# Differential attention in a decoder trunk: the fourth group's values are projected beside its own heads, score halves alternate, sums of squares go inside output units

## The chip, the cores and the metric

The kernel runs on one core of one Trainium2 chip. The metric is the device time of one execution in microseconds (us), lower is better. The engines are named as in the profile: PE (TensorE matmul), PEld (TensorE weight load), DVE (VectorE), ACT (ScalarE), POOL (GpSimd), SP (SyncE, which here issues all the weight DMAs).

## The reference

A trunk of two layers on 256 tokens of width 2048, everything in float32. Layer 0 mixes with sliding-window attention, layer 1 with differential attention; each is followed by cross-attention into 256 memory tokens and a gated MLP with a width-3 convolution. The change lies in the differential attention of layer 1:

```python
def diff_attention(h, w_qkv, w_o, lq1, lk1, lq2, lk2, subln_g, lambda_init):
    qkv = h @ w_qkv                       # 16 heads, two query/key halves of 64 each, values of 128
    q, k, v = jnp.split(qkv, 3, axis=-1)
    ...
        s = jnp.einsum('bqhmd,bshmd->bhmqs', qblk, k) * scale
        s = s - slopes[None, :, None, None, None] * dist
        s = jnp.where(dist >= 0, s, NEG_INF)
        p = jax.nn.softmax(s, axis=-1)
        a = p[:, :, 0] - lam * p[:, :, 1]
        return jnp.einsum('bhqs,bshe->bqhe', a, v)
    ...
    o = rmsnorm(o, subln_g) * (1.0 - lambda_init)   # over the 128 values of a head
    return o.reshape(B, S, DIFF_HEADS * DIFF_V_DIM) @ w_o
```

## The kernel before

Weights stream in **units** of 1 MB (128 partitions x 4 x 512 float32). SP loads unit after unit into four raw slots, ACT copies a unit to its rounded high part (`hi_unit`, L226), DVE subtracts to get the low part (`lo_unit`, L234), and PE multiplies high by high, high by low and low by high (`triple`, L317 to L319). The high and low parts also have four slots: the high part of a unit may be made once the unit four places earlier has been used by PE (`units_used`), and both are made three units ahead of PE (`AHEAD = 3`). A unit is either projected with the weights stationary and 256 tokens streaming (`proj_unit`: queries, keys, output) or with the tokens stationary and 512 weight columns streaming (`token_unit`: values).

The order of the work is written out by hand for each engine, and semaphores tie the engines together. There is no scheduler. Each engine runs its own list strictly from top to bottom, so whatever stands behind an instruction that waits, waits too.

The 16 heads of the differential attention come in four groups of four. After group g's heads follows its **key-value block**: the keys of group g+1 (four units, into the PSUM pair PB), then the values of group g+1 (four units, into PD). Between and beside them:

- *Scores of a head* (`diff_scores`, L941 and L942): for each of the two halves m, on partitions 0 to 63 or 64 to 127, a matmul of 128 columns and one of 256 columns, into PC. Written in the order half 0 (128, 256), half 1 (128, 256).
- DVE adds the distance bias (L1877), takes maxima (L1883, L1884) and negates them (L1888): `diff_bias_max`. ACT takes four exponentials (L1327): `diff_exp`. DVE combines the two softmaxes (L1896 to L1908): `diff_combine`. PE transposes the probabilities (L629): `diff_turn`. ACT moves them to SBUF (L1102): `evac_probs`. PE multiplies by the values (L951 to L953): `diff_pv`. ACT moves the result (L1335): `diff_o_evac`.
- When a group's four heads are done, ACT squares the outputs (L1341), PE sums over partitions with a matrix of ones (L960, `head_norm_sums`), DVE scales the sums (L1916, `diff_norm_first`), ACT takes the root (L1345), DVE takes the reciprocal over 128x1024 (L1920) and multiplies (L1923): `diff_norm_last`. These are placed beside the next keys' units.
- The output projection of group g-1 runs in four output units beside the heads of group g (`o_unit`); DVE adds each to the residual h (L381, `add_block`).
- DVE moves the keys out of PSUM with a scale (L375, `evac_k`) and the values (L1851, L1852, `evac_v`).

Groups 1 and 2 are one hardware loop over g (`Fori(1, 3)`, L999, L1373, L1949). In it `diff_pv(g, 3)` stands right behind `diff_pv(g, 2)`, ahead of the key-value block.

The fourth group (g = 3) is written out. Its heads run beside the output units of group 2, one unit per head. Its own outputs are normalised in two halves of two heads (`half_squares` L1390, `half_norm_sums` L1018, `half_norm_first` L1964, `half_root` L1397, `half_norm_last` L1970 and L1973), split into high and low (`o_hi_half` L1132, `o_lo_half` L1566), and projected by the last four output units, of which `last_part` does a quarter at a time. `last_blocks` then needs the second half.

Of the kernel before, what the change touches and what calls it, by code (L numbers as in the profile page):

```python
# [27 lines left out]
ALU = mybir.AluOpType  # L28
# [3 lines left out]
P = 128  # L32
# [22 lines left out]
AHEAD = 3  # L55
# [6 lines left out]
B_DIFF = B_FF[0] + 3 * FF_STEPS  # L62
# [12 lines left out]
def trunk(nc, x, mem, norm_mix, norm_cross, norm_mem, norm_ffn, norm_final,  # L75
# [4 lines left out]
    with ExitStack() as ctx:  # L80
# [66 lines left out]
        PA, PB, PC, PD = pair  # L147
# [383 lines left out]
        def _(pe):  # L531
# [432 lines left out]
            def diff_turn(g, j):  # L964
                if j == 0:
                    pe.wait_ge(dif["v_evac"], g + 1)
                turn_probs(dif, g, 4, j, pbuf[:, j % 2], THREE)

            def key_value_blocks(g, b4, j0, behind):

                for kq in range(KQ):
                    proj_unit(pe, b4, j0 + kq, PB, xhi, xlo, kq, kq == 0, kq == 3)\
                        .then_inc(units_used, 1)
                    if kq == 0 and behind:
                        diff_turn(g, 3)
                        diff_pv(g, 2)
# [22 lines left out]
            with pe.Fori(1, 3) as g:  # L999
# [10 lines left out]
                diff_pv(g, 3)  # L1010
# [9 lines left out]

            b4 = B_DIFF + 14
            for j in range(3):
                diff_scores(3, j)
                o_unit(dif, 3, b4, j, j, False)
                if j >= 1:
                    diff_turn(3, j - 1)
                if j >= 2:
                    diff_pv(3, j - 2)
            diff_scores(3, 3)
            diff_turn(3, 2)  # L1030
            diff_pv(3, 1)
            diff_pv(3, 2)
            pe.wait_ge(dif["biased"], 16)
            half_norm_sums(0)
            o_unit(dif, 3, b4, 3, 3, False)
            diff_turn(3, 3)
            diff_pv(3, 3)
            half_norm_sums(1)
            last_part(dif, B_DIFF + 15, 0, 0)
            last_part(dif, B_DIFF + 15, 1, 0)  # L1040
            last_part(dif, B_DIFF + 15, 0, 1)
# [7 lines left out]
        def _(act):  # L1049
# [297 lines left out]
            def beside_key_value_blocks(g, b4, j0, behind):  # L1347
                for t in range(8):
                    hi_unit(act, b4, j0 + t + AHEAD)
                    if behind and t == 0:  # L1350
                        evac_probs(dif, g, 4, 3, 3 * P)
                        diff_o_evac(g, 2)
# [20 lines left out]
            with act.Fori(1, 3) as g:  # L1373
# [8 lines left out]
                diff_o_evac(g, 3)  # L1382
                diff_norm(g)
# [16 lines left out]
            heads_with_one_unit(3, b4, 3)  # L1400
# [3 lines left out]
            diff_exp(3, 3)  # L1404
            diff_o_evac(3, 2)
            half_root(0)
            evac_probs(dif, 3, 4, 3, 3 * P)
            diff_o_evac(3, 3)
            o_hi_half(dif, 0)
            half_squares(1)  # L1410
            half_root(1)
            o_hi_half(dif, 1)
            hi_unit(act, b4, 3 + AHEAD)
# [6 lines left out]
        def _(dve):  # L1420
# [428 lines left out]
            def evac_v(g, done):  # L1849
                dve.wait_ge(units_used, done)  # L1850
                dve.tensor_scalar(diff_v[:, 0], PD[:, 0:512], rcol[:, 1, 0:1], None, ALU.mult)  # L1851
                dve.tensor_scalar(diff_v[:, 1], PD[:, 512:1024], rcol[:, 1, 1:2], None, ALU.mult)\  # L1852
                   .then_inc(dif["v_evac"], 1)
# [12 lines left out]
            evac_v(0, 4 * B_DIFF + 12)  # L1866
# [59 lines left out]
            def beside_key_value_blocks(g, b4, j0, q_done, behind):  # L1926
# [5 lines left out]
                for t in range(8):  # L1932
# [8 lines left out]
                evac_v(g + 1, b4 * 4 + j0 + 8)  # L1941
# [7 lines left out]
            with dve.Fori(1, 3) as g:  # L1949
                b4 = g * 4 + (B_DIFF + 2)  # L1950
                for j in range(4):
# [4 lines left out]
                    diff_combine(g, j)  # L1956
                    lo_unit(dve, b4, 2 * j + 1 + AHEAD)
                add_block(dif, b4, 7, PB[:], 3)
# [8 lines left out]
            def half_norm_last(i):  # L1967
                part = q_flat[:, 512 * i:512 * i + 512]
                dve.wait_ge(dif["o_root"], GROUPS + i)
                dve.reciprocal(part, part).then_inc(dif["o_rstd"], 1)  # L1970
                dve.wait_ge(dif["o_rstd"], GROUPS + i)
# [5 lines left out]
            for j in range(4):  # L1977
                diff_bias_max(3, j)
                if j >= 1:
                    add_block(dif, b4, j - 1, pair[(j - 1) % 2][:], j - 1)  # L1980
                if j < 3:
                    lo_unit(dve, b4, j + AHEAD)
                    diff_combine(3, j)
            half_norm_first(0)
            diff_combine(3, 3)
            half_norm_last(0)
            o_lo_half(dif, 0)
            half_norm_first(1)
            add_block(dif, b4, 3, PB[:], 3)
# [49 lines left out]
```

## Time and profile before

Three runs: median 2413.57 us, lowest 2412.19, highest 2415.09.

| | us |
|---|---|
| time of the profiled execution | 2412.89 |
| its span in the profile | 2411.1 |
| PE busy | 2366.2 (98% of the span) |
| DVE busy | 1752.5 (73%) |
| ACT busy | 1183.5 (49%) |
| group 1, first score matmul to group 2's | 101.93 |
| group 2, first score matmul to group 3's | 101.92 |
| group 3, first score matmul to the first output quarter that needs its second half | 44.74 |

In these last three stretches PE is busy for 101.08, 101.07 and 41.12 us, DVE for 72.14, 70.67 and 39.39 us, and the mean granted clock of PE is 1.00, 1.00 and 0.96 of full speed. A timeline row gives start, duration, engine, line, operation, written and read tiles, shape, how many records were merged, and in brackets the idle time of the engine before it with what ended it. The time between the starts of two rows of PE, and not the sum of durations, is what a piece of work costs there, since matmuls overlap in the pipeline.

### The profile page before, as it was taken

To read this page: it belongs to the slowest core of one execution; us is meant where nothing else is said; L and a number is where in the kernel's file an instruction comes from. 1 tells how busy PE (TensorE), PEld (TensorE's weight loads), DVE (VectorE), ACT (ScalarE), POOL (GpSimd) and SP (SyncE) were. 2 spreads that over 40 slices of the span, in tenths; PEclk is the share of its full clock that TensorE was granted. 3 is DMA by queue.
4 is the path that set the end of the run, shared out by engine and by line. 5 is a ranking of instruction groups with operands and counts; after the bars stand their busy time and mean duration, and the time that the engine had idled before them with its cause. 6 is when DMAs were issued, how large, how long until landed. Compare 5 with 4: busy or idle time off the path is not lost.

```text
span 2411.1 us, 36280 instructions
## 1 busy us (share of the span) xinstructions
PE 2366.2 (98%) x14781; PEld 2104.2 (87%) x14781; DVE 1752.5 (73%) x2043; ACT 1183.5 (49%) x1363; POOL 8.6 (0%) x19
## 2 busy tenths in 40 slices
PE   6999999999999999999999999999999999999998
PEld 6898889988888888888899999889888888888887
DVE  5766667777777777777966867787766766676667
ACT  5544446554444444444545444456544444444444
POOL 1000000000000000000000000000000000000000
PEclk9999999999999999999999999999999999999999
DMA  7653433465555555555464544535555555555552
GB/s 260 210 177 106 137 110 120 160 208 192 192 184 194 187 186 189 191 191 192 157 210 158 169 160 160 174 112 180 191 198 187 182 194 188 190 187 196 189 186 96
DMA packets 211928, 424.90 MB, mean 176 GB/s; under 512 B 6896, under 2 KB 7168, under 8 KB 211200
## 3 DMA queue, kind: packets, MB, share of 16 engines
q1 hardware_dynamic: 211152, 421.69, 51.7%
q0 software_dynamic: 688, 1.96, 0.3%
q8 instruction: 66, 1.08, 0.2%
q14 instruction: 22, 0.18, 0.0%
HBM read 421.52 MB, written 2.10 MB: 176 GB/s over the span
## 4 chain that ended last, share of the span: by engine, by line
PE 95%; DVE 3%; ACT 1%; DMA 1%; issue 0%; SPq 0%; ACTq 0%; DVEq 0%
PE pair L343 33%; PE pair L345 17%; PE pair L317 14%; PE pair L319 13%; PE pair L318 13%; DVE wlo L234 1%; PE pair L629 1%; PE pair L620 0%; PE pair L640 0%; PE pair L619 0%; DMA raw<-in_x_w_kv 0%; ACT whi L226 0%; DMA raw<-in_mem 0%; PE pair L641 0%; PE pair L642 0%
## 5 line engine op out<-in xcount | busy, mean ns | idle before, releaser
L234 DVE TENSOR_TENSOR wlo<-raw,whi 128x2048 fp32r<-128x2048 f32 x396 | 905.1, 2288 | 330.1 <-ACT whi L226 329.8
L226 ACT ACTIVATE whi<-raw 128x2048 fp32r<-128x2048 f32 x396 | 756.8, 1914 | 693.5 <-PE pair L345 403.7
L343 PE MATMUL pair<-xx,whi 128*128 128x512 f32 x2880 | 1002.0, 394 | 1.2
L345 PE MATMUL pair<-xx,wlo 128*128 128x256 f32 x2880 | 798.4, 277 | 0.0
L343 PEld LDWEIGHTS pair<-xx,whi 128*128 128x128 f32 x2880 | 540.0, 188 | 130.3 <-issue 5.2
L345 PEld LDWEIGHTS pair<-xx,wlo 128*128 128x128 f32 x2880 | 540.9, 188 | 0.1
L317 PE MATMUL pair<-xx,whi 128*128 128x256 f32 x1184 | 343.2, 290 | 9.9 <-DVE wlo L234 9.1
L318 PE MATMUL pair<-xx,whi 128*128 128x256 f32 x1184 | 336.5, 284 | 0.0
L319 PE MATMUL pair<-xx,wlo 128*128 128x256 f32 x1184 | 336.4, 284 | 0.0
L317 PEld LDWEIGHTS pair<-xx,whi 128*128 128x128 f32 x1184 | 228.6, 193 | 20.3 <-issue 18.7
L318 PEld LDWEIGHTS pair<-xx,whi 128*128 128x128 f32 x1184 | 228.7, 193 | 1.5 <-issue 1.2
L319 PEld LDWEIGHTS pair<-xx,wlo 128*128 128x128 f32 x1184 | 228.6, 193 | 0.0
L343 PE MATMUL pair<-oo,whi 128*128 128x512 f32 x640 | 222.6, 394 | 1.2 <-DVE h L1630 1.2
L345 PE MATMUL pair<-oo,wlo 128*128 128x256 f32 x640 | 177.3, 277 | 0.0
L317 PE MATMUL pair<-oo,whi 128*128 128x256 f32 x512 | 147.7, 289 | 1.0 <-DVE oo L1560 1.0
L343 PEld LDWEIGHTS pair<-oo,whi 128*128 128x128 f32 x640 | 120.0, 188 | 29.4 <-DVE h L1630 1.5
L319 PE MATMUL pair<-oo,wlo 128*128 128x256 f32 x512 | 144.9, 283 | 0.0
L318 PE MATMUL pair<-oo,whi 128*128 128x256 f32 x512 | 144.8, 283 | 0.0
L381 DVE TENSOR_TENSOR h<-h,pair 128x1024 f32<-128x1024 f32 x80 | 97.4, 1217 | 53.0 <-PE pair L319 52.9
L1756 DVE TENSOR_TENSOR work<-pair,work 128x512 f32<-128x512 f32 x88 | 56.7, 686 | 101.5 <-ACT work L1237 101.5
L317 PE MATMUL pair<-whi,oo 128*128 128x512 f32 x320 | 124.6, 390 | 0.0
L319 PE MATMUL pair<-whi,oo 128*128 128x512 f32 x320 | 124.6, 389 | 0.0
(204 smaller groups left out, 2684.2 us busy)
## 6 DMA issues: line engine op xcount, KB each, us to landing
raw<-in_ffn_w_up SPq DMA_DIRECT2D x176, 1024.0 KB, 5.0
raw<-in_ffn_w_down SPq DMA_DIRECT2D x88, 1024.0 KB, 5.0
raw<-in_diff_w_qkv SPq DMA_DIRECT2D x48, 1024.0 KB, 5.1
raw<-in_swa_w_qkv SPq DMA_DIRECT2D x20, 1024.0 KB, 5.1
raw<-in_x_w_kv SPq DMA_DIRECT2D x16, 1024.0 KB, 6.2
raw<-in_swa_w_o SPq DMA_DIRECT2D x16, 1024.0 KB, 5.0
raw<-in_diff_w_o SPq DMA_DIRECT2D x16, 1024.0 KB, 5.0
raw<-in_x_w_q SPq DMA_DIRECT2D x8, 1024.0 KB, 5.5
```

The source lines that it names most:

```text
L226: act.activation(whi[:, s], raw[:, s], ACT.Copy).then_inc(hi_ready, 1)
L234: dve.tensor_tensor(wlo[:, s], raw[:, s], whi[:, s].bitcast(F32), ALU.subtract)\
L317: pe.matmul(dst, ahi, bhi, start=start, stop=False, skip_group_check=True)
L318: pe.matmul(dst, ahi, blo, start=False, stop=False, skip_group_check=True)
L319: return pe.matmul(dst, alo, bhi, start=False, stop=stop, skip_group_check=True)
L343: pe.matmul(banks[m], whi[:, s, k, w], act2[:, c].rearrange("p a t -> p (a t)"), start=c == 0, stop=False, skip_group_check=True)
L345: ins = pe.matmul(banks[m][:, 0:SEQ], wlo[:, s, k, w], act2[:, c, 0], start=False, stop=last and k == 3, skip_group_check=True)
L381: return dve.tensor_tensor(part, part, src, ALU.add)
L629: ins = pe.transpose(pt_ps[:, dst_cols], src[:, src_cols], ident[:])
L1756: ins = dve.tensor_tensor(part, high, part, ALU.add)
```

## The change

1. **Score halves alternate.** The four matmuls of a head's scores are written 128 (half 0), 128 (half 1), 256 (half 0), 256 (half 1).
2. **`diff_pv(g, 3)` moves** from ahead of the key-value block to behind its first key unit for g = 1 and 2; ACT's evacuation and squares move with it. DVE's fourth `add_block` moves one `lo_unit` earlier.
3. **The value units of group 3 leave the key-value block of group 2** and stand beside group 3's first heads: two behind the scores of head 0, two behind the scores of head 1. They go into PB, where the keys of group 3 have been. The key-value block of g = 2 is left with its four key units; its `evac_k` on DVE comes at the end of that shortened block, and the high and low parts of group 2's output (`o_hi_all`, `o_lo_all`) come after it. The wait for the values moves from `diff_turn` to `diff_pv`.
4. **Group 3 is written anew** on PE, ACT and DVE. The two sums of squares stand inside output units 2 and 3, behind the first quarter of each (`o_unit_around_sums`). On ACT, `evac_probs` of head 3 stands behind `o_hi_half(0)`. On DVE, `half_norm_recip` is a function of its own. The last output unit's quarters go 0,0 0,1 1,0 1,1.
5. The loop over g = 1, 2 becomes two written-out copies on the three engines. SP's list is as before.

```diff
@@ pe: diff_scores, diff_pv, diff_turn @@
-                for m in range(2):
-                    half = slice(64 * m, 64 * m + 64)
-                    dst = PC[:, 512 * m:512 * m + 384]
-                    pe.matmul(dst[:, 0:P], q_sb[half, j, Q0], k_sb[half, j, 0:P], start=True, stop=True)
-                    ins = pe.matmul(dst[:, P:3 * P], q_sb[half, j, Q1], k_sb[half, j, :], start=True, stop=True)
+                halves = [slice(64 * m, 64 * m + 64) for m in range(2)]
+                for m, half in enumerate(halves):
+                    pe.matmul(PC[:, 512 * m:512 * m + P], q_sb[half, j, Q0], k_sb[half, j, 0:P], ...
+                for m, half in enumerate(halves):
+                    ins = pe.matmul(PC[:, 512 * m + P:512 * m + 3 * P], q_sb[half, j, Q1], k_sb[half, j, :], ...
...
+                if j == 0:
+                    pe.wait_ge(dif["v_evac"], g + 1)      # in diff_pv
...
-                if j == 0:
+                if j == 0 and g < 3:                      # in diff_turn
                     pe.wait_ge(dif["v_evac"], g + 1)
@@ pe: key_value_blocks and groups 1, 2 @@
+                        else:
+                            diff_pv(g, 3)                 # behind key unit 0
...
+                if g == 2:
+                    return
                 pe.wait_ge(dif["o_evac"], g * 4 + 4)
...
-            with pe.Fori(1, 3) as g:
+            for g in (1, 2):
...
-                diff_pv(g, 3)
                 pe.wait_ge(dif["h_added"], g * 4)
                 key_value_blocks(g, b4, 8, False)
@@ pe: group 3 @@
+            def o_unit_around_sums(nb, i):
+                pe.wait_ge(dif["h_added"], 7 + nb)
+                for k in range(4):
+                    ins = proj_part(pe, b4, nb, pair[nb % 2], ohi, olo, k)
+                    if k == 0:
+                        half_norm_sums(i)
+                ins.then_inc(units_used, 1)
+            diff_scores(3, 0); value_unit(0); value_unit(1); diff_turn(3, 0)
+            diff_scores(3, 1); value_unit(2); value_unit(3)
+            diff_scores(3, 2); diff_turn(3, 1); diff_pv(3, 0); o_unit(dif, 3, b4, 0, 0, False)
+            diff_scores(3, 3); pe.wait_ge(dif["v_evac"], 4); o_unit(dif, 3, b4, 1, 1, False)
+            diff_turn(3, 2); diff_pv(3, 1)
+            pe.wait_ge(dif["biased"], 16)
+            o_unit_around_sums(2, 0)
+            diff_turn(3, 3); diff_pv(3, 2); diff_pv(3, 3)
+            o_unit_around_sums(3, 1)
@@ act: group 3 @@
+            o_hi_all(dif, 2, "o_normed"); hi_unit(act, B_DIFF + 13, 0 + AHEAD); diff_exp(3, 0)
...
+            diff_exp(3, 3)
+            hi_unit(act, b4, 1 + AHEAD)
             evac_probs(dif, 3, 4, 2, 3 * P)
             diff_o_evac(3, 1)
             half_squares(0)
-            diff_exp(3, 3)
+            half_root(0)
+            hi_unit(act, b4, 2 + AHEAD)
+            o_hi_half(dif, 0)
+            evac_probs(dif, 3, 4, 3, 3 * P)
             diff_o_evac(3, 2)
@@ dve: beside_key_value_blocks and group 3 @@
-                for t in range(8):
+                for t in range(4 if g == 2 else 8):
                     lo_unit(dve, b4, j0 + t + AHEAD)
                     if t == (4 if behind else 3):
                         diff_norm_first(g)
                         diff_norm_last(g)
...
-                evac_v(g + 1, b4 * 4 + j0 + 8)
+                if g == 2:
+                    evac_k(g + 1, b4 * 4 + j0 + 4)
+                else:
+                    evac_v(g + 1, b4 * 4 + j0 + 8, PD)
...
+            evac_v(3, 4 * (B_DIFF + 14), PB)
+            diff_bias_max(3, 2); lo_unit(dve, b4, 0 + AHEAD); diff_combine(3, 2)
+            diff_bias_max(3, 3); add_block(dif, b4, 0, PA[:], 0); lo_unit(dve, b4, 1 + AHEAD)
+            diff_combine(3, 3); add_block(dif, b4, 1, PB[:], 1)
+            half_norm_first(0); lo_unit(dve, b4, 2 + AHEAD); half_norm_recip(0); half_norm_last(0)
+            o_lo_half(dif, 0)
```

In the diff, calls that follow one another are put on one line here where they are only a list.

How the instructions stand. First DVE, before, in the loop over groups 1 and 2, beside the key-value block (`ptbuf` holds the variance of the group's heads, the `work` that is written from `pair,rstd` is the next group's keys):

```order
L234 TENSOR_TENSOR wlo<-raw,whi 128x2048
L1916 TENSOR_SCALAR ptbuf<-pair 128x1024
L1920 RECIPROCAL ptbuf<-ptbuf 128x1024
L1923 SCALAR_TENSOR_TENSOR work<-work,subln,ptbuf 128x1024
L233 REGISTER_ALU
L234 TENSOR_TENSOR wlo<-raw,whi 128x2048
L375 SCALAR_TENSOR_TENSOR work<-pair,rstd 128x1024
L233 REGISTER_ALU
L234 TENSOR_TENSOR wlo<-raw,whi 128x2048
```

The same place of DVE in group 2 of the changed kernel, with the first instructions of group 3:

```order
L234 TENSOR_TENSOR wlo<-raw,whi 128x2048 x4
L1957 TENSOR_SCALAR ptbuf<-pair 128x1024
L1961 RECIPROCAL ptbuf<-ptbuf 128x1024
L1964 SCALAR_TENSOR_TENSOR work<-work,subln,ptbuf 128x1024
L375 SCALAR_TENSOR_TENSOR work<-pair,rstd 128x1024
L1918 SCALAR_TENSOR_TENSOR pbuf<-dist_diff,slopes,pair 128x384 x2
```

One `lo_unit` no longer stands between the normalisation and the keys' evacuation, and what follows the evacuation is now group 3's first bias instead of five more units' worth of work.

Second ACT at the end of group 3, before, from the squares of the first half on (L1102 is `evac_probs`, here of head 3, L1132 is `o_hi_half`):

```order
L1397 ACT_TABLE_LOAD
L1397 ACTIVATE work<-work 128x512
L1102 ACTIVATE ptbuf<-pair 128x384
L1335 ACTIVATE work<-pair 128x256
L1132 ACTIVATE xx<-work 128x2x256
L1390 ACTIVATE work<-work 128x512
```

And in the changed kernel (L1425 is `half_root`, L1158 `o_hi_half`, L1128 `evac_probs`, L1361 `diff_o_evac`):

```order
L1425 ACT_TABLE_LOAD
L1425 ACTIVATE work<-work 128x512
L226 ACTIVATE whi<-raw 128x2048
L1158 ACTIVATE xx<-work 128x2x256
L1128 ACTIVATE ptbuf<-pair 128x384
L1361 ACTIVATE work<-pair 128x256 x2
L1418 ACTIVATE work<-work 128x512
```

Head 3's probabilities stood ahead of the high part of the first half's output, and now stand behind it and behind one more weight unit.

## Rows read from the trace of the kernel before

**Rows 1.** The page's busy times of the whole span.
```profile
PE 2366.2 (98%) x14781; PEld 2104.2 (87%) x14781; DVE 1752.5 (73%) x2043; ACT 1183.5 (49%) x1363; POOL 8.6 (0%) x19
```

**Rows 2.** Group 3: stretch, us; PE, PEld, DVE, ACT, POOL busy; PEclk; DMA.
```profile
1548.80:1593.54 44.74, 41.12 (x313) 37.01 (x312) 39.39 (x69) 23.38 (x52) 0.00 (x0) 0.96 0.28 97
```

**Rows 3.** Timeline, end of group 2's heads: start, duration, instruction, [idle before].
```profile
1499.59 1.22 DVE L381 TENSOR_TENSOR h<-h,pair 128x1024 f32<-128x1024 f32 x1 [1.52 <-PE pair L319]
...
1500.16 0.39 PE L953 MATMUL pair<-ptbuf,work 128*128 128x128 f32 x2
...
1502.10 0.36 PE L317 MATMUL pair<-xx,whi 128*128 128x256 f32 x1
```

**Rows 4.** Timeline, from the last key unit's end in group 2's block.
```profile
1526.91 0.40 PE L317 MATMUL pair<-whi,xx 128*128 128x512 f32 x1
...
1527.86 6.55 DVE L1920 RECIPROCAL ptbuf<-ptbuf 128x1024 f32<-128x1024 f32 x1 [1.13 <-ACT ptbuf L1345]
...
1534.45 1.28 DVE L1923 SCALAR_TENSOR_TENSOR work<-work,subln,ptbuf 128x1024 f32<-128x1024 f32 x1
...
1537.85 1.22 DVE L375 SCALAR_TENSOR_TENSOR work<-pair,rstd 128x1024 f32<-128x1024 f32 x1
```

**Rows 5.** Timeline, PE: a window-attention head's scores (one half), then a differential head's.
```profile
277.53 0.48 PE L619 MATMUL pair<-work 64*128 64x128 f32 x2 [0.89 <-DVE sinkg L1526]
277.85 0.59 PE L620 MATMUL pair<-work 64*128 64x256 f32 x2
...
1344.95 0.50 PE L941 MATMUL pair<-work 64*128 64x128 f32 x4
1345.28 0.61 PE L942 MATMUL pair<-work 64*128 64x256 f32 x4
```

**Rows 6.** Timeline, PE: one output unit, turn and product, then group 3's two ends.
```profile
1480.06 0.28 PE L317 MATMUL pair<-oo,whi 128*128 128x256 f32 x1
...
1485.82 0.49 PE L629 MATMUL pair<-ident,pbuf 128*128 128x128 f32 x3
...
1486.91 0.50 PE L941 MATMUL pair<-work 64*128 64x128 f32 x4
...
1548.80 0.50 PE L941 MATMUL pair<-work 64*128 64x128 f32 x4
...
1593.54 0.39 PE L317 MATMUL pair<-xx,whi 128*128 128x256 f32 x1 [0.78 <-DVE xx L1566]
```

**Rows 7.** The page's costliest groups: count, busy, mean ns, idle before, releaser.
```profile
L234 DVE TENSOR_TENSOR wlo<-raw,whi 128x2048 fp32r<-128x2048 f32 x396 | 905.1, 2288 | 330.1 <-ACT whi L226 329.8
L226 ACT ACTIVATE whi<-raw 128x2048 fp32r<-128x2048 f32 x396 | 756.8, 1914 | 693.5 <-PE pair L345 403.7
```

**Rows 8.** Timeline, DVE at the end of group 3.
```profile
1571.54 1.14 DVE L1877 SCALAR_TENSOR_TENSOR pbuf<-dist_diff,slopes,pair 128x384 f32<-128x384 f32 x2
...
1575.98 0.18 DVE L1896 RECIPROCAL stat<-stat 128x4 f32<-128x4 f32 x1
...
1578.19 3.35 DVE L1970 RECIPROCAL work<-work 128x512 f32<-128x512 f32 x1 [0.40 <-ACT work L1397]
1581.58 0.75 DVE L1973 SCALAR_TENSOR_TENSOR work<-work,subln 128x512 f32<-128x512 f32 x1
```

**Rows 9.** Timeline, ACT at the end of group 3.
```profile
1572.25 0.49 ACT L1102 ACTIVATE ptbuf<-pair 128x384 f32<-128x384 f32 x1 [1.21 <-PE pair L629]
...
1574.08 0.40 ACT L1327 ACTIVATE pbuf<-pbuf,stat 128x128 f32<-128x128 f32 x1
...
1575.86 0.36 ACT L1335 ACTIVATE work<-pair 128x256 f32<-128x256 f32 x1
```

**Rows 10.** Timeline, PE: the first projection of the kernel.
```profile
29.24 0.55 PE L317 MATMUL pair<-xx,whi 128*128 128x256 f32 x1 [9.08 <-DVE wlo L234]
```

**Rows 11.** Two stretches, columns as in Rows 2 (DMA share, GB/s last).
```profile
30.00:35.00 5.00, 5.00 (x26) 5.00 (x25) 4.00 (x6) 5.00 (x7) 0.00 (x0) 0.51 1.04 382
...
1584.00:1588.00 4.00, 3.69 (x12) 2.67 (x13) 2.23 (x4) 0.89 (x2) 0.00 (x0) 0.57 0.00 0
```

More of the change, by code:

```diff
@@ L973, in key_value_blocks @@
                         .then_inc(units_used, 1)
-                    if kq == 0 and behind:
-                        diff_turn(g, 3)
-                        diff_pv(g, 2)
+                    if kq == 0:
+                        if behind:
+                            diff_turn(g, 3)
+                            diff_pv(g, 2)
+                        else:
+                            diff_pv(g, 3)
                     if kq == 1:
@@ L1347, in beside_key_value_blocks @@
             def beside_key_value_blocks(g, b4, j0, behind):
-                for t in range(8):
+                for t in range(4 if g == 2 else 8):
                     hi_unit(act, b4, j0 + t + AHEAD)
-                    if behind and t == 0:
-                        evac_probs(dif, g, 4, 3, 3 * P)
-                        diff_o_evac(g, 2)
+                    if t == 0:
+                        if behind:
+                            evac_probs(dif, g, 4, 3, 3 * P)
+                            diff_o_evac(g, 2)
+                        else:
+                            diff_o_evac(g, 3)
+                            diff_norm(g)
                     if behind and t == 1:
@@ L1371, in _ @@
             beside_key_value_blocks(0, B_DIFF + 3, 4, True)
-            with act.Fori(1, 3) as g:
+            for g in (1, 2):
                 b4 = g * 4 + (B_DIFF + 2)
@@ L1865, in _ @@
                     evac_k(0, 4 * B_DIFF + 8)
-            evac_v(0, 4 * B_DIFF + 12)
+            evac_v(0, 4 * B_DIFF + 12, PD)
             def diff_bias_max(g, j):
@@ L1931, in beside_key_value_blocks @@
                 dve.wait_ge(dif["group_ready"], g + 1)
-                for t in range(8):
+                for t in range(4 if g == 2 else 8):
                     lo_unit(dve, b4, j0 + t + AHEAD)
@@ L1947, in _ @@
             beside_key_value_blocks(0, B_DIFF + 3, 4, 4 * B_DIFF + 16, True)
-            with dve.Fori(1, 3) as g:
+            for g in (1, 2):
                 b4 = g * 4 + (B_DIFF + 2)
@@ L1970, in half_norm_last @@
                 dve.reciprocal(part, part).then_inc(dif["o_rstd"], 1)
+            def half_norm_last(i):
+                part = q_flat[:, 512 * i:512 * i + 512]
                 dve.wait_ge(dif["o_rstd"], GROUPS + i)
@@ L1976, in _ @@
             b4 = B_DIFF + 14
[L1977 to L1983, printed above, removed]
+            diff_bias_max(3, 0)
+            o_lo_all(dif, 2)
+            lo_unit(dve, B_DIFF + 13, 0 + AHEAD)
+            diff_combine(3, 0)
+            lo_unit(dve, B_DIFF + 13, 1 + AHEAD)
+            diff_bias_max(3, 1)
+            lo_unit(dve, B_DIFF + 13, 2 + AHEAD)
+            diff_combine(3, 1)
+            lo_unit(dve, B_DIFF + 13, 3 + AHEAD)
+            evac_v(3, 4 * (B_DIFF + 14), PB)
+            diff_bias_max(3, 2)
+            lo_unit(dve, b4, 0 + AHEAD)
+            diff_combine(3, 2)
+            diff_bias_max(3, 3)
+            add_block(dif, b4, 0, PA[:], 0)
+            lo_unit(dve, b4, 1 + AHEAD)
+            diff_combine(3, 3)
+            add_block(dif, b4, 1, PB[:], 1)
             half_norm_first(0)
-            diff_combine(3, 3)
+            lo_unit(dve, b4, 2 + AHEAD)
+            half_norm_recip(0)
             half_norm_last(0)
             o_lo_half(dif, 0)
+            add_block(dif, b4, 2, PA[:], 2)
             half_norm_first(1)
+            half_norm_recip(1)
             add_block(dif, b4, 3, PB[:], 3)
```

66 lines of the change are left out of this document (41 added, 25 removed).

## The prediction

> **What bounds the kernel now.** I read the busy times first: PE is busy for 98% of the span [rows 1], so outside the few waits every microsecond is PE's. Then the stretch of group 3, in which PE is busy for 41.12 of 44.74 us and DVE for 39.39 [rows 2], the one place of the changed region with waits worth naming. Then the timeline of PE through group 3, and of DVE and ACT beside it. The reader should see in them that PE's work is fixed (the change adds and removes no matmul), so the change can only move waits, and that the two engines beside PE have single long instructions: a reciprocal of 6.55 us [rows 4] and one of 3.35 us [rows 8]. Anything PE needs that stands behind one of these on the same engine is late by its whole length. The question for each edit is therefore what now stands behind what.
>
> Prices used below. An output or key unit takes PE 1485.82 - 1480.06 = 5.76 us, a quarter of one 1.44; a turn and a product take 1486.91 - 1485.82 = 1.09 us [rows 6]. Four value units take from 1526.91 [rows 4] to 1548.80 [rows 6], 21.89 us, so 5.47 each. A head's scores take some 0.95 us with their transition [rows 5]. A high part is 1.9 us on ACT and a low part 2.2 to 2.3 on DVE [rows 7]. The bias and the maxima last from 1571.54 [rows 8] to the exponentials at 1574.08 [rows 9], 2.5 us; the exponentials until 1575.86, 1.8 us [rows 9]; the combination from 1575.98 until the 3.35 us reciprocal's idle time of 0.40 began at 1577.79, 1.8 us [rows 8]. Small copies on ACT take 0.36 and 0.49 us [rows 9], and squares, roots and high parts of 128x512 I take at 0.6. A semaphore takes about 0.05 us; I leave it out except where it decides.
>
> **Score halves alternate: 0 us.** A window-attention head's scores use one half of the rows. Its first matmul starts at 277.53 and its last ends at 277.85 + 0.59 = 278.44, 0.91 us. A differential head has twice the matmuls, on both halves, and takes from 1344.95 to 1345.28 + 0.61 = 1345.89, 0.94 us [rows 5]. In the same row all four records of the 128-column matmuls of both halves come ahead of the four of the 256-column ones, although the program writes them half by half. So the two halves already run beside each other, and writing them alternately removes nothing. One bound, if the rows misled me, is a saving of half a head's 0.94, 0.47 us. The other is a loss of 0.1 us a head, the transition that I can't resolve. I take 0, since the two sums from the same rows differ by 0.03.
> The Trainium skill, page "TensorE: Matmul & The Clock Gate", section "Part 2: What happens when you issue a matmul", says that only weight loads are pulled ahead while the matmuls themselves stay in program order. By that rule half 1 would not start until half 0's 256 columns had been issued, and the alternation would be worth something; the trace contradicts it here, since the 128-column matmuls of half 1 start before the 256-column ones of half 0.
>
> **`diff_pv(g, 3)` behind the first key unit: -0.6 us in each of groups 1 and 2.** Before, PE's product of head 2 is at 1500.16, head 3's product waits for its probabilities, and the first key unit starts at 1502.10 behind it [rows 3]. Now the key unit follows head 2's product at once, save that it must wait for the fourth residual addition, which starts at 1499.59 because it needs the last output unit, and lasts 1.22 [rows 3]: the unit starts at 1500.85 at the earliest. The product then costs its own 0.65 us inside the block. 1502.10 - 1500.85 - 0.65 = 0.6. Twice, -1.2. The unit covers head 3's evacuation of 0.49 us ten times over. If this cover went, the old wait would come back and the two gains with it, so one bound is 0; the other is a key unit that needn't wait for the addition, at 1500.3 and so 0.55 more a group, -2.3.
>
> **The loop written out: 0 us.** Group 3 is already written out, and its first scores start at 1548.80, at the end of the loop's last value unit, with no idle time noted [rows 6]. I see no price in either form.
>
> **Keys of group 3: +9.9 us.** Before, the keys' last unit ends at 1526.91 and 21.89 us of values follow, in whose shadow DVE takes its reciprocal (1527.86 to 1534.45), multiplies (to 1535.65), makes one low part (1535.65 to 1537.85) and evacuates the keys from 1537.85 on [rows 4, 6]. Now the value units stand behind head 0's scores, and head 0's scores need the evacuated keys. DVE's list has lost only the one low part between: scaling, reciprocal, multiplication, then the evacuation. So it starts at 1535.65 and takes 1.15 to 1.2, and PE starts the scores at 1536.85 instead of 1526.91: 9.9 us of idle PE with nothing else in its list. DVE can't start the chain earlier, because its fourth low part waits for the high part, which waits for the third key unit; that holds in both kernels. Bounds: 8.8 (if the evacuation ran beside the multiplication's end) and 12.1 (if one low part were still ahead of it). SP's queue is not in this: units are loaded four ahead, and its list is the same.
>
> **Group 3 anew.** I count from the start of head 0's scores, t = 0. PE: scores 0.95, two value units, turn, scores, two value units: t = 24.2. Scores of head 2: 25.1. Meanwhile DVE evacuates the values (two instructions of 0.75, as 128x512 in rows 8) until 25.6, so the product of head 0 waits 0.2 and ends at 26.3. Output unit 0: 32.1. Scores of head 3: 33.0. Output unit 1: 38.8. Turn and product: 39.8. First quarter of output unit 2: 41.3. There PE meets the sums of squares.
> What they wait for is a chain on DVE and ACT from t = 25.6: bias of head 2 to 28.1, exponentials to 29.9, high part (ACT) to 31.8, low part (DVE) to 34.0, combination to 35.8, bias of head 3 to 38.3, exponentials to 40.2, one more high part to 42.1, probabilities, output and squares 0.4 + 0.3 + 0.6 to 43.5. PE waits 2.3 us. Every link of 1.8 to 2.5 us here is from [rows 7, 8, 9].
> Sums and the rest of unit 2: 48.5. Turn of head 3, product of head 2: 49.5. **The product of head 3 needs its probabilities, which on ACT now stand behind `o_hi_half(0)`.** Chain: exponentials of head 3 at 40.2; high part on ACT until 42.1, low part on DVE until 44.4; combination 46.2; residual addition 1.2: 47.4; variance 0.7: 48.0; root on ACT 48.7; high part 50.6; low part on DVE 52.8; reciprocal 3.35: 56.2; multiplication 56.9; high part of the output 57.5; only then probabilities 57.9 and output of head 2 58.3. PE idles from 49.5 to 58.3, 8.8 us. Before, the same probabilities were evacuated ahead of the output's high part, and all the waits of group 3 together were 44.74 - 41.12 = 3.6 us [rows 2].
> After it: product 0.65, output unit 3 with its sums 5.76 + 0.85, four quarters 5.76: t = 71.3, where the first quarter that needs the second half begins. Its low part is ready by then (sums at t = 61, then 0.7 + 0.6 + 3.35 + 1.2 + 0.7 + 0.6 + 0.7 makes t = 69).
> Before, values and group 3 took 21.89 + (1593.54 - 1548.80) = 66.63 us from the keys' end [rows 4, 6]. Now 9.9 + 71.3 = 81.2: +14.6 us.
>
> **The clock of PE: +4.4 us.** After a wait of 9.1 us PE worked from 29.24 on [rows 10], and the granted clock stayed at 0.51 from 30 to 35, the lower of its two levels of 1.2 and 2.4 GHz; in 1584 to 1588 it was 0.57, behind the waits of group 3 [rows 11]. The first cost half of 5.7 us, 2.8; the second half of 3.4 us, 1.7 (this one goes with the old order, and is inside the 66.63). The changed kernel has two waits of about nine us, the length of the first; I take 2.2 for each, between the two. Bounds: 0 and 2.8 each.
>
> **Sum.** From the profiled execution's own time of 2412.89 (span 2411.1): -1.2 + 14.6 + 4.4 = +17.8, so 2430.7. The profiled execution is 0.7 below the median of the three runs, 2413.57.
>
> **The rivals.**
> - *The same waits, but the clock costs nothing.* 2412.89 - 1.2 + 14.6 = 2426.3. For it: no wait of this length lies in the middle of dense work here, so the two rows may not carry over. Against it: both stretches at the lower level followed idle PE.
> - *Alternating halves do gain.* If matmuls did stay in program order, 16 heads times 0.47 is 7.5 us less: 2423.2. The rule named above would give this; [rows 5] speak against it.
> - *More lateness in the chains.* The second chain has some 14 handovers between engines; 0.15 us each, and both clock losses at their upper bound, give +3.3: 2434.0. For it: DVE is busy for 39.39 of 44.74 us in group 3 before [rows 2].
> - *Faster than before.* The mechanism would be DVE's and ACT's lists not holding PE at the two places. Then the waits of group 3 and its clock loss (3.6 + 1.6 us) and the 1.2 go: 2406.5. It decides at a combined wait of 6.4 us; the reciprocal alone, 6.55 us, stands between the keys' projection and their evacuation and is over that. Against it stands the order of DVE's instructions, which leaves no room.
>
> **How the numbers follow.** The forecast has 0.72, the clock rival 0.10, alternating halves 0.06, lateness 0.07, faster or no change 0.05. The forecast's own spread (clock 0 to 5.6, the second wait a microsecond either way) is about 2427 to 2433. The range that should hold 8 in 10 reaches to both sides' cases: 2424 to 2434.5. A difference of 0.2%, 4.8 us, is what a measurement can tell from none. Slower by more than that means above 2418.4: all cases but the last, 0.95. The last I split into faster 0.03 and same 0.02.
>
> **What would show it.** In the profile after: a wait of PE for the keys' evacuation (L375 by DVE) of 9 to 10.5 us ahead of head 0's scores; a wait of 8 to 10 us ahead of one product (released by ACT's output evacuation), and one of about 2.3 us ahead of the sums; the clock at the lower level for some us behind the two long ones; scores of a head still 0.95 us; the old waits ahead of head 3's product gone in groups 1 and 2. I am wrong if the keys' evacuation starts before the reciprocal, or if PE's scores take 0.5 us a head, or if the time is within 5 us of before.

## The result and the profile after

The changed kernel takes 2430.48 us (median of four runs, 2429.89 to 2433.74) against 2413.20 for the kernel before in four runs. The ratio is 1.0074, 95% interval 1.0062 to 1.0086. The forecast was 2430.7. The page of the changed kernel begins with the span and the busy time of each engine:

```profile
span 2428.7 us, 36165 instructions
PE 2369.8 (98%) x14781; PEld 2107.4 (87%) x14781; DVE 1752.7 (72%) x2043; ACT 1182.7 (49%) x1363; POOL 8.5 (0%) x19
```

Against [rows 1] the span is 17.6 us longer and PE is busy for only 3.6 us more; the other 14 us are idle PE. The table of PE's waits says what for (engine and line that waited, engine and line that released it: us in total, times, longest). The rows left out are those of the first microseconds and of layer 0, or have not changed:

```profile
PE pair L940 <- DVE work L375: 9.9, 1, 9.9
...
PE pair L955 <- ACT work L1361: 8.3, 1, 8.3
...
PE pair L1026 <- ACT work L1418: 1.6, 1, 1.6
...
PE pair L317 <- DVE h L381: 0.6, 2, 0.3
PE pair L955 <- DVE work L1893: 0.3, 1, 0.3
```

In the same table of the kernel before, these stood for the groups that the change touches:

```profile
PE pair L951 <- ACT ptbuf L1102: 2.3, 3, 0.9
...
PE pair L1018 <- ACT work L1390: 1.5, 1, 1.5
...
PE pair L317 <- DVE xx L1566: 0.8, 1, 0.8
```

**The keys of group 3.** The timeline of DVE in the changed kernel, at the end of group 2's keys (answers to [rows 4]):

```profile
1523.43 1.22 DVE L1957 TENSOR_SCALAR ptbuf<-pair 128x1024 f32<-128x1024 f32 x1
1525.77 6.55 DVE L1961 RECIPROCAL ptbuf<-ptbuf 128x1024 f32<-128x1024 f32 x1 [1.12 <-ACT ptbuf L1371]
1532.36 1.28 DVE L1964 SCALAR_TENSOR_TENSOR work<-work,subln,ptbuf 128x1024 f32<-128x1024 f32 x1
1533.56 1.22 DVE L375 SCALAR_TENSOR_TENSOR work<-pair,rstd 128x1024 f32<-128x1024 f32 x1
```

and of PE from head 0's scores on (answers to [rows 5, 6]):

```profile
1534.88 0.80 PE L940 MATMUL pair<-work 64*128 64x128 f32 x4 [9.95 <-DVE work L375]
...
1536.46 0.79 PE L317 MATMUL pair<-whi,xx 128*128 128x512 f32 x1
...
1549.69 0.49 PE L629 MATMUL pair<-ident,pbuf 128*128 128x128 f32 x3
1550.11 0.49 PE L940 MATMUL pair<-work 64*128 64x128 f32 x4
...
1550.97 0.50 PE L317 MATMUL pair<-whi,xx 128*128 128x512 f32 x1
...
1562.08 0.49 PE L940 MATMUL pair<-work 64*128 64x128 f32 x4
```

PE stops at 1534.88 - 9.95 = 1524.93, 0.84 us before the reciprocal even starts, and starts again when the evacuation, the second instruction behind the reciprocal, has ended. The first scores take 1536.46 - 1534.88 = 1.58 us and the next head's 0.86; the first two value units take 13.23 us and the next two 11.11.

**The product of head 3.** ACT in the changed kernel, from the high part on that the output's chain waits for:

```profile
1585.69 0.63 ACT L1425 ACTIVATE work<-work 128x512 f32<-128x512 f32 x1 [3.21 <-DVE work L2009]
1586.23 1.89 ACT L226 ACTIVATE whi<-raw 128x2048 fp32r<-128x2048 f32 x1
1594.53 0.63 ACT L1158 ACTIVATE xx<-work 128x512 fp32r<-128x512 f32 x1 [6.41 <-DVE work L2021]
1595.07 0.47 ACT L1128 ACTIVATE ptbuf<-pair 128x384 f32<-128x384 f32 x1
1595.44 0.38 ACT L1361 ACTIVATE work<-pair 128x256 f32<-128x256 f32 x1
```

DVE, from head 2's bias on, with which the chain of [rows 8, 9] begins, and in the 6.41 us for which ACT is idle:

```profile
1563.51 1.13 DVE L1918 SCALAR_TENSOR_TENSOR pbuf<-dist_diff,slopes,pair 128x384 f32<-128x384 f32 x2
...
1588.15 2.29 DVE L234 TENSOR_TENSOR wlo<-raw,whi 128x2048 fp32r<-128x2048 f32 x1 [2.50 <-ACT whi L226]
1590.36 3.35 DVE L2015 RECIPROCAL work<-work 128x512 f32<-128x512 f32 x1
1593.74 0.75 DVE L2021 SCALAR_TENSOR_TENSOR work<-work,subln 128x512 f32<-128x512 f32 x1
```

PE beside it, from the first sums on:

```profile
1581.23 1.13 PE L1026 MATMUL pair<-work,ones 128*128 128x512 f32 x2 [1.60 <-ACT work L1418]
...
1586.50 0.49 PE L629 MATMUL pair<-ident,pbuf 128*128 128x128 f32 x3
...
1587.28 0.39 PE L957 MATMUL pair<-ptbuf,work 128*128 128x128 f32 x2
1595.95 0.77 PE L955 MATMUL pair<-ptbuf,work 128*128 128x128 f32 x2 [8.29 <-ACT work L1361]
```

The probabilities are turned by about 1587 and leave PSUM only at 1595.07, because ACT sits for 6.41 us in front of `o_hi_half(0)`, which stands ahead of them and waits for DVE's multiplication (L2021). DVE spends that time on a low part of a weight unit, on the reciprocal and on the multiplication: the reciprocal alone is 3.35 of the 6.41 us.

**The clock** of the changed kernel (answers to [rows 11]; columns: stretch, length, busy us of PE, PEld, DVE, ACT, POOL, granted clock, DMA share, GB/s):

```profile
1534.88:1541.00 6.12, 6.12 (x19) 4.50 (x20) 4.37 (x9) 4.80 (x10) 0.00 (x0) 0.50 0.00 0
1541.00:1549.69 8.69, 8.69 (x39) 7.11 (x38) 5.31 (x8) 1.92 (x1) 0.00 (x0) 0.99 0.37 123
...
1596.00:1599.61 3.61, 3.61 (x19) 3.61 (x20) 1.01 (x1) 1.01 (x2) 0.00 (x0) 0.56 0.02 5
```

**The whole stretch**, from the last key unit's end to the first quarter that needs the second half. Changed kernel:

```profile
1524.88:1610.53 85.65, 65.55 (x409) 57.33 (x409) 60.56 (x78) 35.20 (x59) 0.00 (x0) 0.88 0.29 98
```

Kernel before:

```profile
1526.91:1593.54 66.63, 63.01 (x410) 54.87 (x408) 58.39 (x77) 32.92 (x58) 0.00 (x0) 0.97 0.36 126
```

The stretch is 19.02 us longer with the same matmuls: 16.48 more of idle PE (20.10 against 3.62) and 2.54 more of busy PE, which is the clock. Groups 1 and 2 give back 1.1 us, and the rest of the 17.6 lies outside the changed region: the changed kernel's profiled execution reaches group 1 1.0 us earlier (1343.98 against 1344.95) and takes 0.6 us more behind the stretch. Executions differ by as much with no change there: group 1 begins at 1342.76 in e6's.

### The profile page after: what moved, and what is told of

Its sections match the earlier page's. It is cut to its first block, busy times and chain, and to the rows that moved or that the text cites. A ratio compares the mean times of both kernels' runs of the same rounds, so it can differ in the third digit from the quotient of the medians.

```text
span 2428.7 us, 36165 instructions
## 1 busy us (share of the span) xinstructions
PE 2369.8 (98%) x14781; PEld 2107.4 (87%) x14781; DVE 1752.7 (72%) x2043; ACT 1182.7 (49%) x1363; POOL 8.5 (0%) x19
## 4 chain that ended last, share of the span: by engine, by line
PE 94%; DVE 3%; ACT 1%; DMA 1%; issue 1%; SPq 0%; ACTq 0%; DVEq 0%
PE pair L343 33%; PE pair L345 17%; PE pair L317 14%; PE pair L319 13%; PE pair L318 13%; DVE wlo L234 1%; PE pair L629 1%; ACT whi L226 1%; PE pair L620 0%; PE pair L619 0%; PE pair L640 0%; DMA raw<-in_x_w_kv 0%; DMA raw<-in_mem 0%; DVE ptbuf L1961 0%; PE pair L641 0%
## 5 line engine op out<-in xcount | busy, mean ns | idle before, releaser
L381 DVE TENSOR_TENSOR h<-h,pair 128x1024 f32<-128x1024 f32 x80 | 97.4, 1218 | 61.2 <-PE pair L319 61.1
```

The lines of the kernel that those rows point to most:

```text
L381: return dve.tensor_tensor(part, part, src, ALU.add)
```

## The experiments

All were run against the kernel before. e1 to e4 edit the changed kernel and shared 7 runs of the kernel before (median 2412.21); e5 and e6 edit the kernel before, e7 and e8 the changed one, and these four shared 29 (median 2412.08). The first four are best compared with each other, above all with `e1`, since they ran on one chip.

**e1: score halves back.** The changed kernel with the old order of the four score matmuls.

```diff
-                for m, half in enumerate(halves): ... 0:P
-                for m, half in enumerate(halves): ... P:3 * P
+                for m in range(2): ... 0:P, then P:3 * P
```

> The changed kernel with the four score matmuls of a head back in their old order. Theory (the two halves ran beside each other before, too): no change against the changed kernel's 2430.5 us, within 1 us, and a head's scores take 0.86 us from their first row to the next unit in both. Rival (alternating halves gained, 0.47 us for each of 16 heads): 7.5 us slower than the changed kernel, 2438, and the slot at 1.3 us.

Measured: 2429.83 us (2428.05 to 2430.91), ratio 1.0074 (1.0057 to 1.0091), the ratio of the changed kernel itself. Its scores of head 1:

```profile
1547.64 0.50 PE L941 MATMUL pair<-work 64*128 64x128 f32 x4
1547.97 0.61 PE L942 MATMUL pair<-work 64*128 64x256 f32 x4
1548.50 0.50 PE L317 MATMUL pair<-whi,xx 128*128 128x512 f32 x1
```

1548.50 - 1547.64 = 0.86 us, as with alternating halves, and here too all records of 128 columns come ahead of those of 256. The order within a head's scores is worth nothing that these runs can tell.

**e2: keys evacuated ahead of the reciprocal.** On DVE only:

```diff
                         diff_norm_first(g)
+                        if g == 2:
+                            evac_k(g + 1, b4 * 4 + j0 + 4)
                         diff_norm_last(g)
...
-                if g == 2:
-                    evac_k(g + 1, b4 * 4 + j0 + 4)
-                else:
+                if g != 2:
```

> The changed kernel, where DVE in group 2 evacuates the keys of group 3 between the scaling of the sums and the reciprocal of 6.55 us. Theory (the keys stood behind the reciprocal): PE's wait of 9.9 us ahead of head 0's scores shrinks to 1.2 us. But head 0's bias now stands behind the same reciprocal, so a new wait of some 3.8 us comes ahead of its turn; about 4.6 us less waiting in sum, and up to 3.0 us less at the lower clock: 2423 to 2426. Rival (the wait is of other origin, e.g. the third variance wait or a late weight unit): the 9.9 us stay, 2430.5. Rival (all of the wait is gained): 2430.5 - 8.7 - 3.0 = 2418.8.

Measured: 2425.93 us (2424.64 to 2427.65), ratio 1.0059 (1.0042 to 1.0076). PE's two waits of this place:

```profile
1526.99 0.49 PE L940 MATMUL pair<-work 64*128 64x128 f32 x4 [1.36 <-DVE work L375]
...
1542.65 0.55 PE L629 MATMUL pair<-ident,pbuf 128*128 128x128 f32 x3 [3.60 <-DVE pbuf L1949]
```

The wait of 9.9 us was the reciprocal: with the evacuation ahead of it 1.36 is left. A new one of 3.60 ends 15 us later, since now the bias and the probabilities of head 0 stand behind the same 6.54 us. 3.9 us are gained over e1, not 8.6; the time is at the upper end of the 2423 to 2426 that was expected.

**e3: head 3's probabilities ahead of the output's high part.** On ACT only:

```diff
             hi_unit(act, b4, 2 + AHEAD)
-            o_hi_half(dif, 0)
             evac_probs(dif, 3, 4, 3, 3 * P)
             diff_o_evac(3, 2)
+            o_hi_half(dif, 0)
             diff_o_evac(3, 3)
```

> The changed kernel, where ACT evacuates head 3's probabilities and head 2's output ahead of the high part of the first half's output, as before the change. Theory (the 8.3 us wait is that order on ACT): the wait ahead of head 3's product falls to about 2 us. The squares of the second half still stand behind that high part on ACT, so a wait of about 5 us appears at the second sums; net 1.9 us, and up to 1.5 us of clock: 2427 to 2428.6. Rival (the whole wait is gained): 2430.5 - 6.3 - 1.5 = 2422.7. Rival (the order on ACT is not the cause): unchanged, 2430.5.

Measured: 2428.76 us (2427.91 to 2430.39), ratio 1.0067 (1.0050 to 1.0084). PE:

```profile
1590.45 0.46 PE L955 MATMUL pair<-ptbuf,work 128*128 128x128 f32 x2 [1.25 <-ACT work L1361]
...
1597.68 2.07 PE L1026 MATMUL pair<-work,ones 128*128 128x512 f32 x2 [4.89 <-ACT work L1418]
```

The product's wait falls from 8.29 to 1.25 us, which names its cause, and 4.89 come back at the second sums: the square of the second half (heads 2 and 3) stands behind `o_hi_half(0)`, as in the changed kernel, and so behind DVE's reciprocal. The waits are 2.2 us shorter in all, the time 1.1 less than e1's, within the spread of the runs and 0.2 above the range that was expected. So it is the wait in the trace that shows the cause here, and not the time. The clock takes part of it: it stays at 0.50 from 1597.68 to 1600 and at 0.60 to 1604, for longer than behind the 8.29 us.

**e4: the keys' wait filled.** Ten matmuls of 512 columns whose result nobody reads stand in PE's list ahead of head 0's scores. They add work to PE and change nothing on the other engines.

```diff
+            for _ in range(10):
+                pe.matmul(PD[:, 0:512], ones[:], rstd[:].rearrange("p a t -> p (a t)"), start=True, stop=True)
             diff_scores(3, 0)
```

> The changed kernel with ten matmuls of 128x512 on constants, whose results nobody reads, written into a free PSUM region ahead of head 0's scores, so that PE works through the wait for the keys instead of idling. They take 10 x 0.85 us and end before the keys are there. Theory (idle PE lowers the clock, which then costs 3.0 us behind the wait: 6.1 us at half speed): the granted clock stays at 1.00 there and the time falls to 2427.5. Rival (the lower clock behind the wait costs nothing on the path, or has another cause): 2430.5. Rival (the matmuls run past the keys' evacuation): slower than 2430.5.

Measured: 2427.33 us (2426.09 to 2429.12), ratio 1.0063 (1.0046 to 1.0080). PE:

```profile
1525.16 8.74 PE L1044 MATMUL pair<-rstd,ones 128*128 128x512 f32 x20
1535.28 0.49 PE L940 MATMUL pair<-work 64*128 64x128 f32 x4 [1.37 <-issue]
...
1536.13 0.50 PE L317 MATMUL pair<-whi,xx 128*128 128x512 f32 x1
...
1547.19 0.49 PE L629 MATMUL pair<-ident,pbuf 128*128 128x128 f32 x3
```

The scores start as late as before, and then take 0.85 us instead of 1.58 and the two value units 11.06 instead of 13.23; the granted clock from 1535.28 to 1541 is 1.00. Adding 8.7 us of work makes the kernel 2.5 us faster than e1. So the loss behind the wait is the clock's.

**e5: the moved product alone.** The kernel before with part 2 of the change (on PE, ACT and DVE), still as a hardware loop:

```diff
-                diff_pv(g, 3)
                 pe.wait_ge(dif["h_added"], g * 4)
                 key_value_blocks(g, b4, 8, False)   # diff_pv(g, 3) behind its key unit 0
```

> The kernel before with edit 2 alone: head 3's product behind the first key unit in groups 1 and 2, and the fourth residual addition one low part earlier. Theory: 0.6 us less in each group, because the key unit must still wait for the addition (0.3 us each): 1.2 us less than before, and PE's waits ahead of the product (0.85 us twice) gone. Rival (the addition doesn't hold the unit): 2.3 us less. Rival (the wait only moves): 0.

Measured: 2410.74 us (11 runs, 2409.44 to 2411.67), ratio 0.9993 (0.9984 to 1.0002). The time alone doesn't settle a microsecond. The trace places it: from group 2's first scores (1445.40) to group 3's (1546.84) are 101.44 us, in group 1 (from 1343.96) the same, against 101.92 and 101.93 before. Half a microsecond a group, a little under the 0.6 that was expected, and a wait of 0.39 us for the addition is left:

```profile
1499.47 0.38 PE L317 MATMUL pair<-xx,whi 128*128 128x256 f32 x1 [0.39 <-DVE h L381]
```

**e6: halves and the written-out loop alone.** The kernel before with parts 1 and 5: the new order within the scores, and `for g in (1, 2)` for `Fori(1, 3)` on PE, ACT and DVE.

```diff
-            with pe.Fori(1, 3) as g:
+            for g in (1, 2):
```

> The kernel before with edits 1 and 5 alone: score halves alternate and the loop over groups 1 and 2 is written out. Theory: neither has a price, so the time is that of before within 1 us, and a head's scores take 0.86 us. Rival (alternating gains 0.47 us a head): 7.5 us faster. Rival (written-out code costs fetches): slower by some us, with gaps of PE in groups 1 and 2.

Measured: 2411.31 us (10 runs, 2409.82 to 2413.01), ratio 0.9999 (0.9989 to 1.0008). Group 2 takes 1546.55 - 1444.65 = 101.90 us, as before. Nothing is left that these runs can tell: the interval of the ratio leaves 2 to 3 us either way for both together, the trace of group 2 a few hundredths. PE has no gap in groups 1 and 2 that the kernel before doesn't have.

**e7: the same idea with no PE wait behind a reciprocal.** Group 3's values are still projected beside its own heads, and the new forms of the sums stay. But DVE's fourth low part of group 2's block, and ACT's high part for it, go behind the normalisation, so the reciprocal starts one low part earlier. The keys' evacuation comes between reciprocal and multiplication, a value unit stands in PE's list ahead of head 0's scores, and the scores run a head ahead of the combinations. The values go into PA, since PB is still being read. The squares of heads 2 and 3 come ahead of `o_hi_half(0)`, and more of PE's work stands between each sum and what it is for. Core of the diff against the changed kernel (PE, then ACT, then DVE):

```diff
+            value_unit(0)
             diff_scores(3, 0)
-            value_unit(0)
             value_unit(1)
-            diff_turn(3, 0)
             diff_scores(3, 1)
             value_unit(2)
-            value_unit(3)
+            diff_turn(3, 0)
             diff_scores(3, 2)
+            value_unit(3)
+            diff_scores(3, 3)
...
             evac_probs(dif, 3, 4, 3, 3 * P)
             diff_o_evac(3, 2)
             diff_o_evac(3, 3)
             half_squares(1)
+            o_hi_half(dif, 0)
...
-                for t in range(4 if g == 2 else 8):
+                for t in range(3 if g == 2 else 8):     # on ACT, too
...
+            diff_norm_first(2)
+            dve.wait_ge(dif["o_root"], 3)
+            dve.reciprocal(ssum, ssum).then_inc(dif["o_rstd"], 1)
+            evac_k(3, (B_DIFF + 13) * 4)
+            norm_mult(2)
```

> A new order of the same instructions, on the changed kernel: the values of group 3 go into PA instead of PB, so that the first value unit needs no evacuated keys and runs ahead of head 0's scores; the other value units stand one behind each head's scores; ACT and DVE lists are arranged so that nothing PE needs next stands behind a reciprocal (head 3's probabilities ahead of the first half's high part, residual additions ahead of the second reciprocal). Theory (all of the loss was waits behind the two reciprocals and the clock behind them, and PE's work itself is fixed): no wait of PE over 1 us from group 2's keys to the cross-attention, clock at 1.00 throughout; the 3.6 us of waits and 1.6 us of clock that the kernel before has in group 3 go too, with the 1.2 us of edit 2: about 7 us faster than before, ratio 0.997. Rival (DVE has too much to do beside these units, and the waits come back spread over many places): about the time of before, ratio 1.000, or slower.

Measured: 2405.40 us (8 runs, 2403.95 to 2406.21), ratio 0.9971 (0.9961 to 0.9982): 6.7 us faster than the kernel before, some 25 than the changed one. In its table of waits one row of group 3 is left:

```profile
PE pair L955 <- DVE work L1901: 0.3, 1, 0.3
```

Busy times and clock from its last key unit to past the end of group 3, columns as above:

```profile
1520.00:1600.00 80.00, 79.74 (x569) 72.33 (x568) 70.31 (x88) 44.00 (x71) 0.00 (x0) 1.00 0.41 139
```

The reciprocal is as long as ever:

```profile
1519.27 6.55 DVE L2039 RECIPROCAL ptbuf<-ptbuf 128x1024 f32<-128x1024 f32 x1 [1.12 <-ACT ptbuf L1377]
1525.94 1.23 DVE L375 SCALAR_TENSOR_TENSOR work<-pair,rstd 128x1024 f32<-128x1024 f32 x1
```

PE beside it:

```profile
1525.74 0.40 PE L317 MATMUL pair<-whi,xx 128*128 128x512 f32 x1
...
1531.30 0.49 PE L940 MATMUL pair<-work 64*128 64x128 f32 x4
```

The last key unit ends and value unit 0 begins at 1525.74. So it is the last key unit that covers the reciprocal here (1519.27 to 1525.82), which in the changed kernel started 0.89 us behind that unit's end. Value unit 0 covers what is left, the evacuation until 1527.17: without it, PE would wait some 1.4 us by these rows (an estimate). Which of the two moves is worth how much was not run by itself.

**e8: a second order of the same kind.** The reciprocal starts as early as in e7, but the keys' evacuation comes behind the multiplication and a low part, and head 3's scores and the last value unit are placed otherwise. The core against e7 (DVE, then PE):

```diff
-            evac_k(3, (B_DIFF + 13) * 4)
             norm_mult(2)
             lo_unit(dve, B_DIFF + 13, 2)
+            evac_k(3, (B_DIFF + 13) * 4)
...
-            value_unit(3)
-            diff_scores(3, 3)
+            value_unit(3)          # ahead of diff_scores(3, 2)
...
+            diff_scores(3, 3)      # behind output unit 0 and diff_pv(3, 1)
```

> Like the previous kernel, but with the reciprocal and multiplication of group 2 ahead of the keys' evacuation, the first two value units around head 0's scores, three products and sums at other places, and the second reciprocal behind the fourth residual addition. Theory: what counts is only that PE has a unit to run while DVE is in a reciprocal, not which of the two orders is taken: also about 7 us faster than before, within 1.5 us of the previous kernel. Rival (the evacuation must come before the reciprocal): a wait of some us ahead of head 0's scores remains.

Measured: 2406.12 us (9 runs, 2404.99 to 2407.72), ratio 0.9975 (0.9966 to 0.9985). The two orders differ by 0.7 us, within their spread. DVE and PE:

```profile
1518.96 6.55 DVE L2039 RECIPROCAL ptbuf<-ptbuf 128x1024 f32<-128x1024 f32 x1 [1.12 <-ACT ptbuf L1377]
1528.95 1.22 DVE L375 SCALAR_TENSOR_TENSOR work<-pair,rstd 128x1024 f32<-128x1024 f32 x1
...
1530.98 0.49 PE L940 MATMUL pair<-work 64*128 64x128 f32 x4
```

The keys are evacuated 3 us later than in e7 and PE still doesn't wait, since value unit 0 lasts until then. One wait that e7 doesn't have is left, for the low part of the second half's output:

```profile
PE pair L317 <- DVE xx L1615: 1.0, 1, 1.0
```

So the evacuation need not come ahead of the multiplication. Both orders start the reciprocal one low part earlier than the changed kernel, so they don't test what happens when a reciprocal starts behind the last key unit.

## Why the prediction was right

| step | forecast, us | measured, us | shown by |
|---|---|---|---|
| score halves | 0 | 0 | e1, e6 |
| product moved, both groups | -1.2 | -1.1 (0.59 in group 1, 0.47 in group 2 up to its keys' end); -1.0 in e5 | trace, e5 |
| loop written out | 0 | 0 | e6 |
| wait for the keys | 9.9 | 9.95 | trace, e2 |
| wait for the values | 0.2 | 0.26 | trace |
| wait for the first sums | 2.3 | 1.60 | trace |
| wait for head 3's product | 8.8 | 8.29 | trace, e3 |
| clock behind the two long waits | 2.2 + 2.2 | 2.9 + 1.6 | trace, e4 |
| PE's own work in the stretch, at the full clock | 60.0 | about 61.1 | trace |

**Which engine holds PE.** The step that carried the forecast was to read the lists of DVE and ACT behind each of PE's waits. e2 moved the evacuation ahead of its reciprocal and e3 moved two copies on ACT ahead of the one that waits for the product of the other reciprocal, and the wait in question fell to 1.36 and 1.25 us. The other side's rival, that nothing is held by those lists, is what e7 had to build: it was worked out as 6.4 us less than before, and e7 took 6.7 less.

**The sizes.** The waits for the sums and the product came out 0.7 and 0.5 us shorter than forecast, and PE's own work 1.1 longer. This is one error and not two that happened to cancel. A wait is what is left of the chain on DVE and ACT when PE's own work is taken off, and the chains were right: from the start of head 2's bias (1563.51, forecast t = 25.6) to the first sums passed 17.7 us where 17.9 were forecast, and to the product of head 3 32.4 where 32.7 were. PE's work beside them was priced too short: 16.4 us for 16.0 from head 1's turn (1562.93) to the sums, and 6.4 for 6.0 from the sums (1581.23) to the end of head 2's product. A part of the latter is a slip in adding up, since the prediction's own prices, 0.85, 4.32 and 1.09, make 6.3. While a chain on the other engines sets the time, such an error moves work into waits and leaves the sum alone. (The window of the stretch has PE busy for 65.55 us, 4.5 of them for the clock; the forecast had 81.2 less its waits of 21.2, so 60.0.)

**The clock** came to 4.5 us against 4.4, but this sum was luck. Behind the 9.95 us wait the scores and two value units took 14.81 us, and 11.91 in e4 at the full clock: 2.9 (the window of 6.12 us at 0.50 says 3.1). Behind the 8.29 us wait PE worked 3.61 us at 0.56: 1.6. The term for each was taken between two rows of before and nothing in them could split it. Nor is its size a property of the wait. In e1's trace the same wait of 9.94 us was followed by 1547.22 - 1533.86 = 13.36 us for the same work, so that execution lost 1.5 there. And behind its second wait, also 8.29 us, it lost 2.4, for the granted clock was 0.55 in the 5.40 us from 1593.60 to 1599.00.

e4's gain of 2.5 over e1 lies between 1.5 and 2.9. Executions of the changed kernel lie between 2429.89 and 2433.74, so that the forecast met the median within 0.2 us is luck as well.

**The rival of the free clock** falls by e4: dummy work of no use would then not have made the kernel faster. e4 and e1 overlap by a microsecond in their runs, but the slots in the rows of e4 leave no doubt. The rival of the alternating halves falls by e1 and e6.

**Not settled.** The gain of the moved product rests on the traces; the interval of e5 just includes no change. The prediction says that DVE can't start the chain of the keys earlier, because its fourth low part waits for a high part that waits for the third key unit. That holds for the two orders it compares, and e7 and e8 show the way round it: with that low part behind the normalisation, the reciprocal starts 6.5 us before the keys' end. The changed kernel with this alone was not run.

## What to carry to other kernels

Before work is pulled out of a block on the critical engine, ask which long instruction of a side engine it was covering: here 22 us of value units hid a 6.55 us reciprocal with the keys' evacuation behind it. Evacuate first what the critical engine waits for next, put long instructions of the side engines where that engine has work that needs nothing of them, and look whether something that can wait itself stands ahead of them, as the fourth low part did here. A fix that moves one instruction out from behind a long one usually puts another behind it (e2, e3), so look at the lists of all engines together: changed together they gave -6.7 us against the kernel before in e7, where e2 and e3 by themselves gave back 4 and 1 of 17.

## What the runs showed of the hardware

- In the records of a head's scores (the one at 1344.95 before, the one at 1547.64 in e1) the matmuls of the two halves of the array's rows start in pairs, 13 or 14 ns apart, with each pair some 0.1 or 0.2 us behind the one ahead of it. Although the program writes 128, 256 (half 0), 128, 256 (half 1), all records of 128 columns come first (e1 and [rows 5]). Written alternately (the head at 1550.11 of the changed kernel) the pairs are 6 or 7 ns apart and the slot is 0.86 us all the same.
- The lower clock followed waits of 8.3 and 9.95 us and also one of 3.60: in e2 the granted clock is 0.65 from 1542.65 to 1545 and 0.82 to 1550. It did not follow the 1.60 us wait of the changed kernel (1.00 from 1581.23 to 1586.5). But the length of one wait doesn't tell: in the kernel before, waits of 0.58 and 1.51 us, within 3 us of each other, have 0.57 behind them ([rows 11], 1584 to 1588). And the loss behind the same wait of the same instructions was 1.5 us in one execution and 2.9 in another, or 1.6 and 2.4.
- RECIPROCAL on DVE takes 6.55 us for 128x1024 in float32 and 3.35 for 128x512, where the scaling of the same 1024 elements (L1957) takes 1.22 and the multiplication (L1964) 1.28.
